# Value products and norm sums in four column groups, in a three-branch block and a two-layer attention model on one core

## The reference

```python
def rms_norm(x, gain=None):
    xf = x.astype(jnp.float32)
    y = xf * lax.rsqrt(jnp.mean(xf * xf, axis=-1, keepdims=True) + EPS)
...
# window attention: probabilities of the window and the context, times the values
o = (jnp.einsum('bnhgqk,bnkhd->bnqhgd', p_win, vb)
     + jnp.einsum('bnhgqk,bkhd->bnqhgd', p_ctx, v_ctx))
...
# differential attention: two maps mixed, times the values
pd = p[:, :, 0] - lam * p[:, :, 1]
return jnp.einsum('bhqk,bkhd->bqhd', pd.astype(v.dtype), v)
```

## Time and profile before

| | |
|---|---|
| median of three runs | 1747.1 us |
| the profiled execution's own time | 1742.35 us |
| its span, first to last instruction | 1740.6 us |
| TensorE busy, matmul records | 1669.4 us (96%) |
| VectorE, ScalarE, GpSimd busy | 1228.0, 867.0, 204.3 us |
| mean granted TensorE clock | 0.983 |
| DMA | 259.80 MB, mean 149 GB/s |

### The profile page before, as it was taken

The page is one execution under the profiler, slowest core; times in us unless marked ns, Lnnn a source line. Parts: engine busy times, 40 slices in busy tenths (PEclk is TensorE's granted clock), DMA queues, the critical chain, the costliest instruction groups (busy, mean ns, idle before and its releaser), DMA issues.

```text
span 1740.6 us, 29999 instructions
## 1 busy us (share of the span) xinstructions
PE 1669.4 (96%) x12542; PEld 1510.1 (87%) x12542; DVE 1228.0 (71%) x2058; ACT 867.0 (50%) x1295; POOL 204.3 (12%) x126
## 2 busy tenths in 40 slices
PE   6999999999999999999899999999999998899999
PEld 5999888898999999998867888888887886799999
DVE  3287479687767886577765788876888678458864
ACT  4433545548546665445655344323433455556653
POOL 4402550000000110100000111100110100041100
PEclk9999999999999999999999999999999899999999
DMA  6656355454445554521101333364344322045544
GB/s 267 227 220 218 148 216 194 170 218 170 146 173 175 187 179 150 186 74 50 73 0 50 121 130 137 138 233 148 122 171 158 126 77 94 1 147 193 184 165 137
DMA packets 41111, 259.80 MB, mean 149 GB/s; under 512 B 4368, under 2 KB 7568, under 8 KB 14480
## 3 DMA queue, kind: packets, MB, share of 16 engines
q1 hardware_dynamic: 40976, 257.88, 40.8%
HBM read 256.82 MB, written 1.05 MB: 148 GB/s over the span
## 4 chain that ended last, share of the span: by engine, by line
PE 76%; DVE 16%; ACT 3%; DMA 2%; issue 2%; POOL 0%; SPq 0%; DVEq 0%; ACTq 0%
PE acc_psum L197 21%; PE acc_psum L199 21%; PE acc_psum L198 21%; DVE w_low_sb L163 3%; PE acc_psum L2458 3%; PE acc_psum L2411 2%; PE acc_psum L2437 2%; DVE mod_products L306 2%; DVE ring_sb L306 1%; DVE u_filtered L1964 1%; DMA ring_sb<-in_w_in 1%; PE acc_psum L242 1%; ACT w_high_sb L152 1%; DMA ring_sb<-in_w_up 1%; PE acc_psum L387 1%
## 5 line engine op out<-in xcount | busy, mean ns | idle before, releaser
L197 PE MATMUL acc_psum<-h_high_sb,w_high_sb 128*128 128x256 f32 (+1 forms) x2176 | 667.9, 307 | 12.5 <-DVE h_low_sb L454 4.3
L199 PE MATMUL acc_psum<-h_high_sb,w_low_sb 128*128 128x256 f32 (+1 forms) x2176 | 660.9, 304 | 0.0
L198 PE MATMUL acc_psum<-h_low_sb,w_high_sb 128*128 128x256 f32 (+1 forms) x2176 | 660.9, 304 | 0.0
L152 ACT ACTIVATE w_high_sb<-ring_sb 128x1024 fp32r<-128x1024 f32 (+2 forms) x412 | 386.8, 988 | 399.3 <-PE acc_psum L199 246.2
L163 DVE TENSOR_TENSOR w_low_sb<-ring_sb,w_high_sb 128x1024 fp32r<-128x1024 f32 (+1 forms) x356 | 388.5, 1133 | 144.1 <-ACT w_high_sb L152 134.0
L197 PEld LDWEIGHTS acc_psum<-h_high_sb,w_high_sb 128*128 128x128 f32 x2176 | 414.9, 191 | 39.7 <-issue 16.5
L198 PEld LDWEIGHTS acc_psum<-h_low_sb,w_high_sb 128*128 128x128 f32 x2176 | 414.9, 191 | 17.5 <-issue 0.5
L199 PEld LDWEIGHTS acc_psum<-h_high_sb,w_low_sb 128*128 128x128 f32 x2176 | 414.6, 191 | 16.9
L163 POOL TENSOR_TENSOR w_low_sb<-ring_sb,w_high_sb 128x1024 fp32r<-128x1024 f32 x56 | 136.9, 2467 | 719.3 <-ACT w_high_sb L152 719.3
L1964 DVE SCALAR_TENSOR_TENSOR u_filtered<-acc_psum,par_sb,u_filtered 128x255 f32<-128x255 f32 (+2 forms) x264 | 150.7, 571 | 59.8 <-ACT u_filtered L2101 41.5
L197 PE MATMUL acc_psum<-u_high,w_high_sb 128*128 128x256 f32 (+1 forms) x528 | 169.0, 320 | 3.2 <-DVE w_low_sb L163 2.5
(11 more groups left out here) (303 smaller groups left out, 1925.5 us busy)
## 6 DMA issues: line engine op xcount, KB each, us to landing
ring_sb<-in_w_in SPq DMA_DIRECT2D x68, 1024.0 KB, 6.3
ring_sb<-in_w_up SPq DMA_DIRECT2D x66, 1024.0 KB, 4.9
ring_sb<-in_w_down SPq DMA_DIRECT2D x48, 704.0 KB, 4.1
ring_sb<-in_w_ada SPq DMA_DIRECT2D x24, 1024.0 KB, 4.8
ring_sb<-in_w_ada_rows SPq DMA_DIRECT2D x24, 1024.0 KB, 4.8
ring_sb<-in_w_out SPq DMA_DIRECT2D x12, 1024.0 KB, 4.8
ring_sb<-in_w_br_hg SPq DMA_DIRECT2D x4, 1024.0 KB, 7.0
ring_sb<-in_w_br_ml SPq DMA_DIRECT2D x4, 1024.0 KB, 4.8
```

Source lines behind the costliest of these rows:

```text
L152: self.nc.scalar.activation(self.high[:, g % 2, piece], self.ring[:, c % RING, piece], ACT.Copy)\
L197: nc.tensor.matmul(out, sh, mh, start=start, stop=False)
L198: nc.tensor.matmul(out, sh, ml, start=False, stop=False)
L199: return nc.tensor.matmul(out, sl, mh, start=False, stop=stop)
```

## The change

A new function `column_groups` makes one product as four matmuls, each with 32 of the 128 stationary columns and the same moving operand, each in its own column group and into its own 32 PSUM partitions; start and stop flags are the same for all four, and the last matmul is returned, on which the caller hangs its signal. It is called in three places: `pair_sums`, `folded_sums` and `values`. Operands, order, waits and signals are otherwise as before. One product of 128 stationary columns so turns from one matmul instruction into four: 240 value products and 90 norm sums are made.

```diff
--- before.py
+++ after.py
@@ -199,6 +199,15 @@
     return nc.tensor.matmul(out, sl, mh, start=False, stop=stop)
 
 
+def column_groups(nc, out, stationary, moving, start, stop):
+
+
+    for c in range(0, P, 32):
+        mm = nc.tensor.matmul(out[c:c + 32, :], stationary[:, c:c + 32], moving, start=start, stop=stop, skip_group_check=True,
+                              tile_position=(0, c))
+    return mm
+
+
 def linker(eng, signal):
 
     start = signal.total
@@ -384,9 +393,8 @@
             for t in (2 * p, 2 * p + 1):
                 w = core.ones[:, 0:1] if st.weights is None else st.weights[:, t:t + 1]
                 for b in range(ST):
-                    mm = core.nc.tensor.matmul(core.psum[:, self.bank, 2 * k + b:2 * k + b + 1], st.v(t)[:, b * P:(b + 1) * P], w,
-                                               start=(k == 0 and t == 0 and b == 0),
-                                               stop=(k == len(self.streams) - 1 and t == DT - 1 and b == ST - 1), skip_group_check=True)
+                    mm = column_groups(core.nc, core.psum[:, self.bank, 2 * k + b:2 * k + b + 1], st.v(t)[:, b * P:(b + 1) * P], w,
+                                       k == 0 and t == 0 and b == 0, k == len(self.streams) - 1 and t == DT - 1 and b == ST - 1)
         if p == DT // 2 - 1:
             mm.then_inc(*self.summed.one())
 
@@ -395,8 +403,8 @@
         core = self.core
         pe.wait_ge(*folded.at(1))
         for b in range(ST):
-            mm = core.nc.tensor.matmul(core.psum[:, self.bank, b:b + 1], self.streams[0].v(0)[:, b * P:(b + 1) * P], core.ones[:, 0:1],
-                                       start=(b == 0), stop=(b == ST - 1), skip_group_check=True)
+            mm = column_groups(core.nc, core.psum[:, self.bank, b:b + 1], self.streams[0].v(0)[:, b * P:(b + 1) * P], core.ones[:, 0:1],
+                               b == 0, b == ST - 1)
         mm.then_inc(*self.summed.one())
 
     def root(self, act, *biases):
@@ -2455,8 +2463,7 @@
                             o_, v_ = psum[:, 7, 65 * m:65 * m + 65], bv1[:, k0 // P + kt, m, :]
                         else:
                             o_, v_ = psum[:, 7, 0:64], cv[:, k0 // P + kt, 64 * h:64 * h + 64]
-                        mm = nc.tensor.matmul(o_, ET[:, u % 2, m, kt * P:(kt + 1) * P], v_, start=(kt == 0),
-                                              stop=(kt == nk // P - 1), skip_group_check=True)
+                        mm = column_groups(nc, o_, ET[:, u % 2, m, kt * P:(kt + 1) * P], v_, kt == 0, kt == nk // P - 1)
                 mm.then_inc(*ov.one())
 
             def first_part(st):
```

## The result

| | before | after |
|---|---|---|
| median, first comparison | 1748.59 us (1745.53 to 1750.77, 4 runs) | 1719.78 us (1716.06 to 1724.92, 4 runs) |
| ratio | | 0.984 [0.981, 0.987] |
| executions of all comparisons whose clock is on record | mean 1745.9 us, 60 | mean 1721.9 us, 13 |
| mean granted clock over those | 0.9811 | 0.9840 |
| the profiled execution, its span | 1742.35 us, 1740.6 us | 1716.06 us, 1714.3 us |

The kernel became faster by 28.8 us in the first comparison and by 24.0 us between the means of the second row (24.2 if the first comparison's four executions of the kernel before, which have no clock on record, are counted too). The forecast was 18.7 us.

A forecast was written before the change was run, and what follows sets the result against it. TensorE was taken as the bound, with 76% of the span hanging on it. Norm sums -7.6, value products in projections -1.6 and in tails -9.5 sum to -18.7: from 1747.1 to 1728.4 us, range 1722 to 1739 (8 in 10).

The forecast's parts named there:

- a round at 64 or 65 columns, at 1: Four column-group matmuls side by side on TensorE: 0.06 us with 65 moving columns, 0.034 with 32 and less.
- 4 records in passing; 8; 16 in the tail: Value-product bursts by old record count, without a wait before: +0.13, -0.09 and -0.50 us each.
- two in the out projection; one behind the earlier trace: Norm-sum bursts: two in layer 0's out projection save 1.9 us; one before layer 1's attention, beside a table load, about 0.6.
- C units of layer 0: Value products in the projections, bursts of 8 and 4 records: together -1.6 us, given for both layers in one sum.
- C units of layer 1, and its tail: Value products in projections and attention tail: -1.6 us and -9.5 us, each given for both layers together.
- short steps: Short value bursts in the tails: five give 0, since TensorE's next transposes start right after ScalarE's exponentials.
- a clock step more or less: Listed among the unknowns that spread the forecast over 1722 to 1735 us, without a size of its own.
- (a): Loads don't hide behind other rounds' streams at 65 columns, a round is 0.03 + 0.057: about 1739 us; chance 0.10.
- (b): Tails' gain handed back because ScalarE's loop or VectorE's reads are longer; norms and projections stay, -9.2: 1738 us; chance 0.08.
- (c): Smaller pieces make TensorE look idle in the attention tails, granted 1.2 instead of 2.4 GHz: up to +42 us; chance 0.04.
- (d): Column groups don't run side by side, so a round costs four times 0.06 or 0.034: about 1833 us; chance 0.01.
- (e): Narrow records have their own floor, eight take what two took, 0.028 each; only fixed prices remain: 1769 us; chance 0.01.

The follow-up runs named there:

- after_again: The changed kernel measured a third time, unaltered, beside the kernel before: 1720.42 us (5 runs), ratio 0.987.
- repeat_after: The changed kernel measured once more, unaltered, beside the kernel before on one chip: 1722.11 us (4 runs), ratio 0.986.

## Why the prediction came out as it did

**Right: the direction, the mechanism and nearly each size that it priced.** By its own steps:

| step | forecast | measured |
|---|---|---|
| a round at 64 or 65 columns, at 1 | 0.06, 0.034 | 0.059, 0.035 |
| burst of 8 at 793.79 | 0.81 | 0.78 |
| norm burst at 682.11 | 0.85 | 0.83 |
| 4 records in passing; 8; 16 in the tail | +0.13; -0.09; -0.50 | +0.11; -0.12; -0.54 |
| five norm bursts ahead of layer 0's attention | 5.1 | 6.7, with 1.6 of clock: 5.1 |
| two in the out projection; one behind the earlier trace rows | 1.9; 0.6 | 1.9; 0.7 |
| C units of layer 0, 783 to 885 | 0.5 | 1.1 |
| layer 0's tail | 5.3 | 4.6 to 5.2 |
| C units of layer 1, and its tail, 1415 to 1520 | 1.1 + 4.2 | 5.2 |
| short steps | 0 | 0 |
| norms alone, values alone | 7.6, 11.1 | 9.8, 15.1 |

The forecast gave both layers in one sum; it is split here by where the bursts stand. The 1.1 of layer 0's C units is `after_again`, which has nearly the half-clock time of the trace of before there, and the 5.2 is `repeat_after`, which has the same 10.2 us as the trace of before from 1415 to 1520. Small errors partly cancel: layer 1's tail alone (1485 to 1520, full clock in both traces) gained 4.8 and not 4.2, because a burst of sixteen gains 0.54 and not 0.50 and the last two, one behind the other, gained 1.37 together; the stage with the C units ahead of it gained 0.4. In layer 0 the three short bursts behind a wait gained 0.16 to 0.21 each and not 0.07.

**Wrong: the total, because the clock was entered as spread and not as a term.** The step that failed is "a clock step more or less" in the unknowns, and ahead of it the sum, which charged every burst at the clock of its own moment. Over all executions before and after, the mean granted clock rose from 0.9811 to 0.9840. Within one kernel the time of an execution falls by 1.57 us for each 0.001 of mean clock, by a line through the executions of this study, so 0.0029 is worth about 4.5 us. At equal clock the change gives some 19.5 us, for a forecast of 18.7. The traces say nearly the same: if half of each us at half clock is lost, by estimate, the three of the changed kernel come out 20 to 21 us under the first of before.

Of the 4.5 us the one norm burst accounts for about 1.6, shown both ways. The rest stays open. In the table it does not lie in layer 1, where the two kernels have about as much half clock (10.2 and 13.7 us from 1415 to 1520 before; 13.6, 10.2 and 13.7 after), but between 783 and 937: 10.2 and 17.1 us before; 3.4, 6.8 and 10.2 after. The stretch at 863 is a part of it. Two and three traces with this scatter don't show that the value products caused it.

The bursts and the clock together make the 24.0. The first comparison showed 28.8 by chance: its four executions of the changed kernel average 1720.1, which is 1.8 below the mean of thirteen, and its four of before average 1748.4, 2.5 above the mean of 60; medians for means account for the rest. The range, too, was drawn from the unknowns of the sum and left out that two medians of few executions can each be off by 2 to 3 us. It ended at 1722 where the mean over thirteen lies at 1721.9.

**The rivals.** (a) fell: rounds of 0.059 where it needed 0.087. The rule of the Trainium skill cited there (a load overlaps a running matmul only in another row group) does not hold for column groups in these traces, which all use the same rows. The round with one column, which is the load, takes 0.035, and the one with 64 or 65 columns 0.059, less than such a load and a stream of 0.057 (an estimate, a quarter of the 0.23 of the earlier trace rows) one behind the other. (b) fell: the tail step above is TensorE alone in the chain, six such steps of layer 1 became 0.47 to 0.55 shorter, and (b) would have left 1738. (c) had the right subject and the wrong sign: in the tail from 1455 to 1520 the changed kernel has a granted clock of 0.91 in one trace and 0.97 in another, and before 0.92 and 0.89, so no loss is seen there, and elsewhere the clock rose. The rows, which take in the end of layer 1's projections and its tail; the changed kernel, first and second trace:

```profile
1455.00:1520.00 65.00, 55.62 (x883) 44.64 (x884) 29.98 (x71) 37.26 (x62) 19.87 (x8) 0.91 0.18 59
```

```profile
1455.00:1520.00 65.00, 57.10 (x874) 45.61 (x874) 34.28 (x79) 36.20 (x59) 17.87 (x8) 0.97 0.19 64
```

and the kernel before, its first and second trace:

```profile
1455.00:1520.00 65.00, 54.44 (x377) 44.85 (x378) 38.65 (x95) 35.92 (x62) 0.00 (x0) 0.92 0.10 33
```

```profile
1455.00:1520.00 65.00, 53.29 (x364) 42.73 (x363) 38.78 (x97) 37.08 (x62) 0.00 (x0) 0.89 0.09 33
```

The same 65 us hold different parts of the program, since the changed kernel is ahead by then; the rows tell only that the smaller pieces are not met with a lower clock. (d) and (e) fell with the same rounds: in the norm burst 32 records start within 0.28 us, less than 0.009 each, so eight take 0.07. The 60 cycles a matmul of the Trainium skill's "TensorEngine Tiling (Array Packing)", "Instruction Overhead", would make 0.20 of eight, by the forecast's estimate, if they ran one behind another. Four ran side by side here, and the change divides the 128 stationary columns, not the small dimension of which that section warns.

## What to carry to other kernels

A product with few moving columns is bound by the load of its 128 stationary columns (0.112 us each here), and four column groups take that to a third with one moving column and to half with 65; two groups of 64 do as well where 64 or 65 columns move (a burst of 1.04 against 1.02). Against it stands a fixed price of about 0.31 (one column) to 0.37 us (64 columns) for each burst that changes the form and changes it back, so a burst of value products gains only from about six of the old records on (four lose 0.11, eight gain 0.12), and an order that saves a change of form is worth 0.18 us only if it doesn't bring the burst ahead of what it waits for. Before the sum is called done, look at the granted clock right behind each burst that is to change, give the clock a term of its own, and compare the mean clock of all executions, not only the profiled ones.

## What was not expected of the hardware

One burst of sixteen one-column records after 1.18 us of idling, 1.8 us from its first record to the next product, decided whether TensorE had 1.2 or 2.4 GHz for 3.4 us right behind it: the granted clock over 735 to 741 is 0.72 with it and 1.00 with the same sums in four column groups, in a kernel that differs in nothing else. Two groups of 64 left the stretch at 1.2 GHz in place (0.89 over 15 us in the window around it), although they are faster than the old form. And one program's executions differ by up to 14.4 us (1737.53 to 1751.89 for the kernel before in one comparison), most of it following the mean granted clock.
